# The up projection of a ConvGLU as block products of halves, in one block with the down projection

## The reference

```python
h = x + hybrid_mixer(rms_norm(x, norm1_w), ...)      # w_o is its last product
x = h + conv_glu_ffn(rms_norm(h, norm2_w), w_up, ffn_conv_w, ffn_conv_b, w_down)
return rms_norm(x, final_norm_w)

def conv_glu_ffn(xn, w_up, conv_w, conv_b, w_down):  # D_FF = 2816
    h = causal_dwconv(xn @ w_up, conv_w) + conv_b    # 3 taps
    gate, val = jnp.split(h, 2, axis=-1)
    return (jax.nn.silu(gate) * val) @ w_down
```

## Time and profile before

| | us |
|---|---|
| three runs, median (lowest to highest) | 1834.77 (1832.7 to 1835.59) |
| the profiled execution, with its span | 1833.01 (1831.3) |
| PE busy in the span | 1705.4 |
| DVE, ACT, POOL busy | 682.2, 497.2, 515.7 |

### The profile page before, as it was taken

How to read it: one execution, slowest core, us unless ns; L and a number is a source line. 1 busy time by engine, 2 the same in 40 slices (tenths; PEclk the granted TensorE clock), 3 DMA queues, 4 the chain that set the end, 5 groups by cost and what they waited for, 6 DMA issues and landing times. The chain is left out here.

```text
span 1831.3 us, 21149 instructions
## 1 busy us (share of the span) xinstructions
PE 1705.4 (93%) x8339; PEld 1412.0 (77%) x8339; DVE 682.2 (37%) x938; ACT 497.2 (27%) x619; POOL 515.7 (28%) x315
## 2 busy tenths in 40 slices
PE   6999879999999999999799969999999999799996
PEld 4788658877778788777588848888888888688885
DVE  4233124444534545333351323222332223244545
ACT  4322211122222233334212222222222222222233
POOL 4335223222121231222024332222222222344444
PEclk9999989999999999999899979999999999899998
DMA  4222312221212123244553111111111111311113
GB/s 152 70 80 81 99 51 73 68 62 31 76 28 70 43 54 100 85 133 128 211 204 131 58 58 46 54 49 46 46 46 56 47 46 34 120 51 47 47 51 120
DMA packets 173546, 139.64 MB, mean 76 GB/s; under 512 B 20420, under 2 KB 153004, under 8 KB 173484
## 3 DMA queue, kind: packets, MB, share of 16 engines
q1 hardware_dynamic: 173120, 138.15, 24.4%
q10 hardware_dynamic: 364, 0.61, 0.1%
HBM read 106.39 MB, written 32.34 MB: 76 GB/s over the span
## 5 line engine op out<-in xcount | busy, mean ns | idle before, releaser
L401 PE MATMUL acc<-xh,w_high 128*128 128x512 f32 x1504 | 491.1, 407 | 7.9 <-PEq L1365 7.9
L401 PE MATMUL acc<-xl,w_high 128*128 128x512 f32 x1504 | 471.3, 394 | 0.0
L401 PE MATMUL acc<-xh,w_low 128*128 128x512 f32 x1504 | 469.5, 393 | 0.0
L401 PEld LDWEIGHTS acc<-xl,w_high 128*128 128x128 f32 x1504 | 285.9, 190 | 62.0
L401 PEld LDWEIGHTS acc<-xh,w_low 128*128 128x128 f32 x1504 | 285.1, 190 | 62.3
L401 PEld LDWEIGHTS acc<-xh,w_high 128*128 128x128 f32 x1504 | 272.5, 191 | 62.3 <-issue 15.5
L1719 DVE SCALAR_TENSOR_TENSOR u_conv<-acc,prm,u_conv 128x1023 f32<-128x1023 f32 x88 | 112.8, 1282 | 341.0 <-ACT u_conv L1682 334.6
L769 POOL TENSOR_TENSOR w_low<-w_raw,w_high 128x1024 fp32r<-128x1024 f32 x49 | 117.3, 2395 | 398.4 <-ACT w_high L843 398.4
L1706 POOL TENSOR_TENSOR w_low<-w_raw,w_high 128x1024 fp32r<-128x1024 f32 x42 | 101.0, 2405 | 363.0 <-ACT w_high L1664 363.0
L1858 DVE TENSOR_TENSOR w_low<-w_raw,w_high 128x512 fp32r<-128x512 f32 x42 | 104.1, 2478 | 130.0 <-ACT w_high L1822 130.0
L1843 POOL TENSOR_TENSOR xl<-glu,xh 128x1024 fp32r<-128x1024 f32 x44 | 105.3, 2394 | 156.6 <-ACT xh L1819 131.4
(11 more groups left out here) (287 smaller groups left out, 2181.2 us busy)
## 6 DMA issues: line engine op xcount, KB each, us to landing
w_raw<-in_w_in_dram SPq DMA_DIRECT2D x51, 512.0 KB, 4.5
w_raw<-in_w_up_dram SPq DMA_DIRECT2D x44, 512.0 KB, 3.8
w_raw<-in_w_down_dram SPq DMA_DIRECT2D x44, 256.0 KB, 2.6
conv_d<-so SPq DMA_DIRECT2D x16, 512.0 KB, 3.0
gate_d<-qk SPq DMA_DIRECT2D x16, 512.0 KB, 3.1
g_gates<-gate_d SPq DMA_DIRECT2D x8, 1024.0 KB, 5.5
qk<-in_x_dram SPq DMA_DIRECT2D x8, 512.0 KB, 8.6
ckqk<-conv_d SPq DMA_DIRECT2D x8, 512.0 KB, 4.6
```

What stands on the lines that cost most here:

```text
L401: mm = nc.tensor.matmul(out[:, lo:hi], w, xx[:, lo:hi], start=first and j == 0, stop=last and j == 2)
```

## The change

- **Up as seven products for eight.** For each i the four blocks of weights (gate and value columns, first and second half of the contraction: A11, A12 | A21, A22) and the four blocks of xn (halves of the contraction, halves of the tokens: B11, B21, T1.., B22) are combined by sums: S1 to S4 of weights, T1 to T4 of xn. Seven products P1 to P7 of 4 x 3 = 12 matmuls of 512 columns give the four output blocks (c11, c12: gate, first and second half of the tokens; c21, c22: value), after further sums. P2 goes into bank X, P1, P6, P7, P4 accumulate in Y (two in turn), P5, P3 in Z (two in turn).
- **Order.** PE works P1(i+1), P4(i), P2(i+1), P3(i), P6(i+1), P5(i+1), P7(i+1) and so on.
- **Per tile on the other engines.** DVE: four weight sums of 512 columns, c11, c12, c22 (each PSUM plus a snapshot in SBUF), two taps for each half of the value (the second half out of the SBUF copy vc), two gate taps of 1024 columns out of the SBUF copy gc, and glu. ACT: three snapshots of PSUM, a copy of two columns, the taps 0 in three pieces, silu, seven splits. POOL: seven low parts of 512 columns, in the order of ACT's splits.
- **Raw weights** have two slots (the ring's and u_raw), a tile's two loads of 512 KB each.
- **glu** keeps four tiles; SP stores tiles 0 to 17 to DRAM (glu_d) behind the wait for each, and loads them again into the place of xn's forms and others, two in flight, after the last P5 (the first 8) and the last P3 (the others). w_down tiles 0 and 1 are issued ahead of them, 2 to 5 behind them, then h, then the rest. Down starts with glu tiles 18, 19, 20, then 0 to 17, then 21.
- **One block** for up and down; all loops are written out.
- **Second norm.** The norm weight is loaded as a row (n2w) and multiplied in the scaling (1024 columns, two tensors); high and low parts are taken straight from PSUM; token tiles go in the order 0, 4, 1, 5, 2, 6, 3, 7, since the sums T take a tile of each half. Five DVE instructions and seven splits make a pair's forms, POOL four of the lows. DVE's low of an even tile replaces POOL's.
- **Head.** Of the eight loads of x, four are in flight: each later one waits for the fourth before it.

The core of the diff: sequence and tables; ACT, POOL and DVE in the second norm; then SP, ACT, DVE and PE in the new block (a split's low on POOL follows each split).

```diff
+PRODUCTS = {"P1": ("A11", "B11"), "P2": ("A12", "B21"), "P6": ("S2", "T2"), "P5": ("S1", "T1"), "P7": ("S3", "T3"),
+            "P4": ("A22", "T4"), "P3": ("S4", "B22")}
+def up_sequence():
+    seq = [(p, 0) for p in ("P1", "P2", "P6", "P5", "P7")]
+    for i in range(FT):
+        more = i + 1 < FT
+        for p, own in (("P1", 1), ("P4", 0), ("P2", 1), ("P3", 0), ("P6", 1), ("P5", 1), ("P7", 1)):
+            if more or not own:
+                seq.append((p, i + own))
+    return seq
...
+SPLIT_AT = {"P1": ("A11",), "P2": ("A12",), "P7": ("S2", "S1", "S3"), "P4": ("A22",), "P3": ("S4",)}
...
+KEPT = 4
...
+                for n in range(NT):
+                    square(n)
+                    if n >= 2:
+                        split_tile(n - 2)
+                split_tile(NT - 2)
+                split_tile(NT - 1)
...
+                def row_factor(n):
+                    pool.wait_ge(s_ms, R0 + n + 1)
+                    nc.gpsimd.tensor_tensor(rstd[:, n:n + 1], ms[:, n:n + 1], mhalf[:, 0:1],
+                                            ALU.pow).then_inc(s_rstd, 1)
+                def lows(p):
+                    for f in SUMS:
+                        pool.wait_ge(s_high, 7 * p + HI[f])
+                        nc.gpsimd.tensor_tensor(forms(p)[f][1], t_sum[f], forms(p)[f][0].bitcast(F32),
+                                                ALU.subtract).then_inc(s_tlo, 1)
+                for n in range(NT):
+                    row_factor(n)
+                    if n >= 3 and n % 2:
+                        lows(n // 2 - 1)
+                lows(NT // 2 - 1)
...
+                def split_tile(n):
+                    p = n // 2
+                    if n % 2 == 0:
+                        dve.wait_ge(s_high, 7 * p + HI["first"])
+                        cols = slice(p * P, (p + 1) * P)
+                        nc.vector.tensor_tensor(xl[:, :, cols], tp[n], xh[:, :, cols].bitcast(F32),
+                                                ALU.subtract).then_inc(s_form, 1)
+                        return
+                    first, last = tp[n - 1], tp[n]
+                    dve.wait_ge(s_high, 7 * p + HI["mid"])
+                    if p:
+                        dve.wait_ge(s_tlo, 4 * p)
+                    nc.vector.tensor_tensor(t_sum["T1"], mid, first[:, 0:KH, :], ALU.subtract).then_inc(s_form, 1)
+                    dve.wait_ge(s_high, 7 * p + HI["B22"])
+                    nc.vector.tensor_tensor(t_sum["T3"], last[:, KH:KT, :], mid, ALU.subtract).then_inc(s_form, 1)
+                    dve.wait_ge(s_form, 6 * p + MADE["T1"])
+                    nc.vector.tensor_tensor(t_sum["T2"], last[:, KH:KT, :], t_sum["T1"], ALU.subtract).then_inc(s_form, 1)
+                    dve.wait_ge(s_form, 6 * p + MADE["T2"])
+                    nc.vector.tensor_tensor(t_sum["T4"], first[:, KH:KT, :], t_sum["T2"], ALU.subtract).then_inc(s_form, 1)
+                    hi, lo = forms(p)["B22"]
+                    nc.vector.tensor_tensor(lo, last[:, KH:KT, :], hi.bitcast(F32), ALU.subtract).then_inc(s_form, 1)
...
+                for n in range(NT):
+                    dve.wait_ge(s_mm, n + 1)
+                    add(1, ORD[n], n)
+                    if n >= 2:
+                        split_tile(n - 2)
+                    dve.wait_ge(s_sq, R0 + n + 1)
...
+                        load_columns(sp, raws[i % 2][:, j], w_up2[:, i * P + j * FF:i * P + j * FF + P], u_raw[i % 2])
...
+                def load_down(kk):
+                    half, t = kk // FT, order[kk % FT]
...
+                    else:
+                        sp.wait_ge(f_wlo, kk - 1)
+                    sp.dma_start(w_raw[kk % 2], w_dn2[t * P:(t + 1) * P, half * HALF:(half + 1) * HALF]
+                                 ).then_inc(f_raw[kk % 2], 16)
+                load(1)
+                for p, i in seq:
+                    if p == "P4" and i + 2 < FT:
+                        load(i + 2)
+                    if p == "P7" and i >= 1 and i - 1 < FT - KEPT:
+                        sp.wait_ge(s_glu, i)
+                        sp.dma_start(glu_d[i - 1], G[:, (i - 1) % KEPT, :]).then_inc(s_gst[(i - 1) % KEPT], 16)
+                    if (p, i) == ("P5", FT - 1):
+                        load_down(0)
+                        load_down(1)
+                for j in range(KEPT):
+                    sp.wait_ge(s_gst[j], 16 * len(range(j, FT - KEPT, KEPT)))
+                sp.wait_ge(s_p, made[("P5", FT - 1)])
+                for t in range(2 * KH):
+                    sp.dma_start(place[t], glu_d[t]).then_inc(s_gin[t % 2], 16)
+                    if t and t < FT - KEPT - 1:
+                        sp.wait_ge(s_gin[(t + 1) % 2], 16 * ((t + 1) // 2))
+                sp.wait_ge(s_p, made[("P3", FT - 1)])
+                for t in range(2 * KH, FT - KEPT):
+                    sp.dma_start(place[t], glu_d[t]).then_inc(s_gin[t % 2], 16)
+                    if t < FT - KEPT - 1:
+                        sp.wait_ge(s_gin[(t + 1) % 2], 16 * ((t + 1) // 2))
+                for kk in range(2, 6):
+                    load_down(kk)
                 for st in range(NT):
                     sp.dma_start(h[st], h_d[st * P:(st + 1) * P, :].rearrange("p (a c) -> p a c", a=NHALF)).then_inc(s_h, 16)
...
+                for kk in range(6, NK):
+                    load_down(kk)
...
+                def split(f, i):
+                    if f in w_sum:
+                        act.wait_ge(s_wsum, 4 * i + SUM_NO[f])
+                    else:
+                        act.wait_ge(u_raw[i % 2], 32 * (i // 2 + 1))
+                    nc.scalar.activation(wf[f][0], source(f, i), ACT.Copy).then_inc(u_whi, 1)
...
+                def high(kk):
+                    j, t = kk % 2, order[kk % FT]
...
+                    elif kk >= 2:
+                        act.wait_ge(s_k, kk - 1 - (kk > FT))
+                    elif kk:
...
+                    if t >= FT - KEPT:
+                        act.wait_ge(s_glu, t + 1)
+                    else:
+                        act.wait_ge(s_gin[t % 2], 16 * (t // 2 + 1))
+                    nc.scalar.activation(gh[j], place[t], ACT.Copy).then_inc(s_gh, 1)
+                    act.wait_ge(f_raw[j], 16 * (kk // 2 + 1))
+                    nc.scalar.activation(w_hi[j], w_raw[j], ACT.Copy).then_inc(f_whi, 1)
+                for f in ("S2", "S1", "S3", "A22", "S4"):
+                    split(f, 0)
+                for p, i in seq:
+                    act.wait_ge(s_p, made[(p, i)])
+                    if p == "P1":
+                        if i:
...
+                    if p == "P6":
+                        if i:
...
+                            act.wait_ge(s_c12, i)
+                        snapshot(u2, Y[i % 2])
...
+                        if i:
...
+                        snapshot(u3, Y[i % 2])
+                    if p == "P5" and i:
...
+                        act.wait_ge(s_g, 2 * i)
...
+                        nc.scalar.activation(sg[:], cv[:, 0, :], ACT.Silu).then_inc(s_silu, 1)
+                    if p == "P4":
...
+                        nc.scalar.activation(vc[:, 0:2], Y[i % 2][:, HALF - 2:HALF], ACT.Copy)
+                        nc.scalar.activation(cv[:, 1, 0:HALF], Y[i % 2], ACT.Identity, bias=bias(1, i),
+                                             scale=tap(1, i, 0)).then_inc(s_tv0, 1)
+                        act.wait_ge(s_c22, i + 1)
+                        nc.scalar.activation(cv[:, 1, HALF:S], vc[:, 2:HALF + 2], ACT.Identity, bias=bias(1, i),
+                                             scale=tap(1, i, 0)).then_inc(s_tv1, 1)
+                    if i + 1 < FT:
+                        for f in SPLIT_AT.get(p, ()):
+                            split(f, i + 1)
+                    if p == "P3":
+                        act.wait_ge(s_c12, i + 1)
+                        nc.scalar.activation(cv[:, 0, :], gc[:, 2:S + 2], ACT.Identity, bias=bias(0, i),
+                                             scale=tap(0, i, 0)).then_inc(s_tg, 1)
+                    if (p, i) == ("P7", FT - 1):
+                        high(0)
+                act.wait_ge(s_g, 2 * FT)
+                act.wait_ge(s_glu, FT - 1)
...
+                nc.scalar.activation(sg[:], cv[:, 0, :], ACT.Silu).then_inc(s_silu, 1)
+                for kk in range(1, NK):
+                    high(kk)
...
+                def weight_sums(i):
+                    dve.wait_ge(u_raw[i % 2], 32 * (i // 2 + 1))
+                    if i:
+                        dve.wait_ge(u_wlo, split_no[("S4", i - 1)])
+                    g.tensor_tensor(w_sum["S1"], block_of("A21", i), block_of("A22", i), ALU.add).then_inc(s_wsum, 1)
+                    dve.wait_ge(s_wsum, 4 * i + 1)
+                    g.tensor_tensor(w_sum["S2"], w_sum["S1"], block_of("A11", i), ALU.subtract).then_inc(s_wsum, 1)
+                    g.tensor_tensor(w_sum["S3"], block_of("A11", i), block_of("A21", i), ALU.subtract).then_inc(s_wsum, 1)
+                    dve.wait_ge(s_wsum, 4 * i + 2)
```

(77 more changed lines are left out.)

632 lines of the change are left out of this document (299 added, 333 removed).

## The result

The changed kernel takes 1846.9 us (median; 1843.6 to 1848.8), the kernel before 1834.3 on the same chip: a ratio of 1.0067, 95% interval 1.0050 to 1.0085. It is slower by 0.7%, or 12.6 us; forecast were +5 and 1840 us. The profiled execution spans 1847.0 us against 1831.3.

A forecast was written before the change was run, and what follows sets the result against it. PE was taken to bound the kernel (93% of the span, 465 of 465 us in up). Up -2.7, up to down +3.4 and second norm +4.3 made +5 on 1833.0, 1838.0; with 1.8 to the median, 1840 us, range 1797 to 1863.

The forecast's parts named there:

- likeliest case: In up, 22.0 to 22.9 us a tile, putting the kernel at 1833 to 1848 us; chance 0.40.
- The ring: In up, raw tile's landing to glu, its store, then the next load's landing: 22.4 us a tile against PE's 19.04.
- Up as a whole: Up takes 478 us against 480.7 before, -2.7, with 17 tiles at 22.4 us.
- PE's two waits: In each round of up, PE waits for ACT's snapshots ahead of P7 and ahead of P4; no size given.
- Taps: In up, DVE's 512-column taps from SBUF are stretched by POOL to a mean near 1.4 us instead of 0.75.
- The step called uncertain: In up, a scalar_tensor_tensor waits for POOL, 2.6 us on the chain; without it the loop would be 19.8.
- Up to down: First steps of down: second step at U+10.4, third at U+25.0 (U: end of up); +3.4 us, bounds 0 and +8.
- Rival C: Before down, the glu reload is far slower than its rows: at 5 us a load, 1853 us; chance 0.05.
- The gap "of some 14": In down, the second of PE's two gaps, until w_raw number 2 lands, some 14 us; the first some 5.
- Second norm: Behind the second norm's products, up starts at 1087.3 instead of 1083.0: +4.3 us, bounds 0 and +7.
- rival B's worst case: In up, POOL wins at glu too, store's 1.5 us ahead of the pair: 24.6 a tile, 1877 us; rival's chance 0.22.
- The break-even of 22.1 us a tile: In up's loop, below 22.1 us a tile the kernel is faster than before, above it slower.

## Why the prediction came out as it did

The direction and the mechanism of up were right, the time was 7 us short, and the likeliest case's own range (to 1848) holds it. Piece by piece, in the profiled spans, up came out 4.2 us longer than forecast and the way into down 9.0 longer, the second norm 2.2 shorter and the head 0.5 shorter: 10.5 in all. So part of the closeness is luck, errors of opposite sign and a profiled pair that lay 3.1 further apart than the medians. By its steps:

- **The ring.** Forecast 22.4 us a tile, measured 22.53, and it binds from tile 4 on as said. Inside, two errors of opposite sign. From landing to glu: 16.35 forecast, 15.3 measured. POOL's blocks were 1.05 at the value taps, 1.0 at the gate taps and 0.5 at glu, 2.55 for the forecast 3.35, and the unblocked part 12.8 for 13.0. From glu to the next split: 6.1 forecast, 6.9 to 8.4 measured, 7.2 in the mean. That was the mis-sized term: the pair takes 5.9 to land, not the 4.7 of the earlier trace rows, and 0.7 of it is the store in front, which I had put at 0.2. The Trainium skill's fit ("SBUF — State Buffer", section "The DMA setup-cost knee"), 5.6 us for store and pair as an estimate, was lower still; the trace does not bear it out here.
- **Up as a whole.** 478 forecast, 482.2 measured: 2.2 from the pace, 0.4 from the slow clock at the start (72 matmuls to the first P4 took 18.6 us, 2.3 over full clock, for 1.9), 0.45 from a second tile of 19.49, 0.8 from a wait at the last P4.
- **PE's two waits.** Two were forecast; nearly all of PE's waiting is in one place, ahead of P7. Ahead of P4 it waited 0.24, not a share worth naming. The slower clock in up, 0.96, was not in the forecast; in the ring's 17 tiles it cost nothing, as the run with less matmul work shows.
- **Taps.** Forecast a mean near 1.4 us instead of 0.75, measured 1.30 (the earlier trace rows showed no such instruction under POOL's load); with POOL away 0.88. The step called uncertain held.
- **Up to down, the step that failed.** Forecast: third step at U+25.0; measured U+34.9. The reload began 0.9 sooner than said, took 36.5 us to the weight's issue for the forecast 28.6, and that weight needed 6.0 from issue to split for 3.1; 7.9 + 2.9 - 0.9 = 9.9. I had put a pair of reads at one landing time of 3.4; each landed in 4.4 with two in flight. The page of before had it already: no 512 KB read on it landed in 3.4, and one that reads back what the kernel had stored took 4.6.

```profile
w_raw<-in_w_up_dram SPq DMA_DIRECT2D x44, 512.0 KB, 3.8
...
ckqk<-conv_d SPq DMA_DIRECT2D x8, 512.0 KB, 4.6
```

  The 3.4 had been worked out from a smaller load and from a store. Rival C had the right place with a higher price (5 a pair, 1853), and the measured 4.3 lies between it and my case. Its reasons, data just written and a queue shared with w_down, were not tested; the run with four in flight shows that the number in flight held the reload back. The same fit of the Trainium skill gives 4.4 as an estimate for a pair of 1.05 MB, and for two in flight the trace agrees: with it the sum would have come to an estimated 1848. For four in flight it does not: 2.1 MB would be an estimate of 6.8, and four loads took 5.1. The second step's 5.0 was measured as 4.95. The gap "of some 14" among the prediction's signs does not follow from its own sum: 14.1 is both gaps together, so the second should have read 9.2, against 17.2 measured.
- **Second norm.** +4.3 forecast, +2.1 measured from the norm's first add to the first product of up (68.2 us against 66.1). Of the nine other profiles with this norm seven have 69.0 to 69.2 and two 66.6. In the two the last eight transposes among the products took 1.09 us, full clock; in the seven 1.97, and the products behind them ran slow as well; so the 2.5 between the two groups is PE's clock. In the changed kernel's own profile the transposes took 1.09 and only the products behind them were slow (granted clock 0.67 over the 4 us from the transposes on), hence 68.2, between the two. The first products of up came at 1084.6, not 1087.3. The last transposes end 65.3 us after the products' start, where I had 67: the splits of the third pair were done 1.3 sooner.
- **Head.** Taken at nothing: the norm's first add came 0.5 us sooner than before, inside the spread between profiles.

Two readings in the prediction are loose, and nothing measured hangs on them: POOL's 2.41 beside the PSUM taps of the earlier trace rows does not lie inside DVE's 2.71 but starts 0.9 later and ends 0.6 later, and rival B's worst case adds up to 24.4 from its own terms (or to 25, if the block at glu is added whole), not 24.6.

The break-even of 22.1 us a tile was right for a +7.7 elsewhere; with +14 elsewhere it would have been 21.7. The run with the store's bytes behind the pair has just that pace, 21.71, and 0.9998 of before.

Open stays why in four of 18 rounds the pair lands 1.1 to 1.5 later. It is regular and not chance: these are the 8th, 11th, 14th and 17th round, 68 us apart, and the same rounds are late in the runs with the weights of down first and with four reloads in flight. In three of the four an instruction load of 16 KB falls between glu and the split, but so it does in two rounds that are not late.

## What to carry to other kernels

When a change adds a store, a load and vector work to a loop that one engine paces, draw the ring first: which load waits for which result, and what stands behind the wait for that load on its in-order engine. Lay out that ring's time; if it is longer than the pacing engine's round, the loop runs at the ring's length, however much work was taken off that engine. Opening the ring at one place (the load ahead of the store, or the wait behind the work) was worth 58 us here, shortening its parts 30 and 13. Ask of every bulk reload how many transfers are in flight before pricing it by bandwidth, and what small urgent load stands behind it in the queue.

## What the runs showed of the hardware

- Reads of 512 KB on SP's queue landed in 4.4 us each with two in flight (232 GB/s) and in 5.1 with four (397 GB/s, DMA share 1.01): twice the depth gave 1.7 times the rate.
- A DVE instruction with both tensors in SBUF and a POOL instruction on SBUF stretch each other: the value taps 0.88 to 1.30 in the mean, the gate taps 1.28 to 1.72, and POOL's 512-column low from 1.28 to 1.72 and, beside glu, 2.27. The PSUM taps stayed at 0.75.
- After a wait of 2.3 to 2.5 us, PE's next twelve matmuls took sometimes 3.0 and sometimes 4.5 us, after 3.8 us 5.4; the granted clock of up fell from 1.00 to 0.96.
